# An encoder layer with product-key experts: the dense tokens' queries and scores move from the f32r scores stage to 16 f32 tiles at the head of the expert phase

## What is computed

```python
q = (h @ wq).reshape(nb, L, 8, 256)                 # 8 heads
q1, q2 = q[..., :128], q[..., 128:]
s1 = einsum('blhd,kd->blhk', q1, keys1)             # 128 keys each
s2 = einsum('blhd,kd->blhk', q2, keys2)
v1, i1 = top_k(s1, 16); v2, i2 = top_k(s2, 16)
cand = v1[..., :, None] + v2[..., None, :]          # 256 sums
sc, ci = top_k(cand, 16)
e = i1[ci // 16] * 128 + i2[ci % 16]                # expert of 16384
w = softmax(sc)
act = gelu(einsum('td,tjd->tj', h, u_tab[e]))       # 8 x 16 experts a token
y = einsum('tj,tjd->td', w * act, v_tab[e])
```

## Time and profile before

| | |
|---|---|
| median of 3 runs | 3317.74 us (3316.46 to 3320.41) |
| the profiled execution | 3320.53 us |
| its span in the profile | 3318.8 us |
| TensorE busy | 2949.9 us, 89% |
| VectorE busy | 2375.7 us, 72% |
| ScalarE, GpSimd busy | 545.1 us, 16%; 1227.4 us, 37% |
| DMA | 909.23 MB, mean 274 GB/s |
| mean granted TensorE clock | 0.939 |

### The profile page before, as it was taken

The page is one execution under the profiler, slowest core; times in us unless marked ns, Lnnn a source line. Parts: engine busy times, 40 slices in busy tenths (PEclk is TensorE's granted clock), DMA queues, the critical chain, the costliest instruction groups (busy, mean ns, idle before and its releaser), DMA issues. The chain is left out here.

```text
span 3318.8 us, 31146 instructions
## 1 busy us (share of the span) xinstructions
PE 2949.9 (89%) x10524; PEld 1623.4 (49%) x10524; DVE 2375.7 (72%) x4478; ACT 545.1 (16%) x652; POOL 1227.4 (37%) x1104
## 2 busy tenths in 40 slices
PE   6999689669699769898999999997799999999995
PEld 2457577547488424444444444443344444444442
DVE  4795454621588899999989988876577676776774
ACT  3011443311211112212212221220000000000003
POOL 0111111022111353334444455554465455555560
PEclk8998899779799779999999999999899999999997
...
GB/s 188 177 161 23 58 39 26 32 58 127 45 83 67 229 305 316 342 336 331 365 373 363 370 368 414 413 413 410 389 403 400 401 402 400 402 399 402 400 381 148
DMA packets 296804, 909.23 MB, mean 274 GB/s; under 512 B 26832, under 2 KB 76240, under 8 KB 293584
## 3 DMA queue, kind: packets, MB, share of 16 engines
...
...
## 5 line engine op out<-in xcount | busy, mean ns | idle before, releaser
L1441 PE MATMUL s_pu<-s_hn,s_ut 128*128 128x512 f32 x2048 | 906.6, 599 | 0.0
L1397 POOL DMA_INDIRECT s_slot<-in_u,s_row x512 | 514.8, 1006 | 625.7 <-DVE s_slot L1761 503.8
L1397 POOL DMA_INDIRECT s_slot<-in_v,s_row x512 | 560.1, 1094 | 489.3 <-DVE s_hB L1774 333.3
L1761 DVE SCALAR_TENSOR_TENSOR s_slot<-s_slot,s_ph 128x1024 f32<-128x1024 f32 x512 | 609.0, 1220 | 112.5 <-DMA s_slot<-in_u,s_row 95.6
L1774 DVE SCALAR_TENSOR_TENSOR s_hB<-s_slot,s_dot,s_hB 128x1024 f32<-128x1024 f32 x445 | 561.4, 1284 | 129.0 <-DMA s_slot<-in_v,s_row 128.1
L1441 PEld LDWEIGHTS s_pu<-s_hn,s_ut 128*128 128x128 f32 x2048 | 393.1, 193 | 482.4 <-issue 482.4
L296 PE MATMUL s_ps<-hn_hi,w_hi 128*128 128x512 f32 x832 | 340.9, 410 | 93.5 <-PEq L270 57.2
L297 PE MATMUL s_ps<-hn_lo,w_hi 128*128 128x512 f32 x832 | 332.2, 399 | 0.0
L1513 PE MATMUL s_pw<-s_ct,s_vt 128*128 128x512 f32 x512 | 250.2, 613 | 37.2 <-DMA s_vt<-in_v 20.5
L300 PE MATMUL s_ps<-hn_hi,w_lo 128*128 128x512 f32 x832 | 261.9, 397 | 0.0
L1513 PE MATMUL s_ph<-s_ct,s_vt 128*128 128x512 f32 x512 | 242.6, 597 | 19.5 <-DVE s_slot L1761 19.5
...
## 6 DMA issues: line engine op xcount, KB each, us to landing
s_ut<-in_u_tiles SPq DMA_DIRECT2D x128, 512.0 KB, 7.3
s_vt<-in_v SPq DMA_DIRECT2D x128, 512.0 KB, 24.0
s_g<-s_gst ACTq DMA_DIRECT2D x128, 256.0 KB, 7.0
...
```

The source lines that it names most:

```text
L1397: pool.indirect_dma_start(out=slot[s][:, :], out_offset=None, in_=io[kind], in_offset=bass.IndirectOffsetOnAxis(ap=row[b][:, j:j + 1], axi ...
L1441: mm = pe.matmul(pu[:, n % 2, :], ut[n % UR][:, k, :], hn[:, k, :], start=(k == 0), stop=(k == DC - 1))
L1761: dve.scalar_tensor_tensor(s, s, 1.0, ph[:, :], ALU.mult, ALU.mult, accum_out=dot[b][:, j:j + 1]).then_inc(taken, 1)
```

## The change

`project` gets `halves`; the scores stage calls it with half 0 alone, so that queries, scores, stores and VectorE's copies cover the 512 gathering tokens only. `MADE_PICKS` falls from 4 to 2: in the scores stage VectorE makes the picks of blocks 0 and 1. The queries of the dense tokens are computed at the head of the first expert phase: `QT` = 16 more tiles, n = -16 to -1, use the rings, PSUM and semaphores of the u tiles with `wq` as the weight (plain f32, 8 matmuls). ScalarE copies a query out (`dense_query`), TensorE multiplies its four blocks with the keys (`dense_scores`, one tile later), ScalarE copies and stores the scores (`take_scores`). SP's loads of scores wait until these 16 stores have landed. The blocks are ranked in another order, and the tables of numbers that set rates and places are new. The last eight steps of block 1's ranking, one a tile, lie in tiles -12 to -5.

```diff
@@ -291 +291 @@
-def project(pe, out, w_hi, w_lo, x_hi, x_lo, ks=range(DC)):
+def project(pe, out, w_hi, w_lo, x_hi, x_lo, ks=range(DC), halves=range(2)):
@@ -294 +294 @@
-        for h in range(2):
+        for h in halves:
@@ -1023,2 +1023,3 @@
-    q = [at(f"s5_q{s}", [P, T], F32, F0 + s * 4 * KB) for s in range(2)]
-    sc = at("s5_sc", [P, 2, NB, KEYS], F32, F0 + 8 * KB)
+
+    q = [at(f"s5_q{s}", [P, HALF], F32, F0 + s * 4 * KB) for s in range(2)]
+    sc = at("s5_sc", [P, 2, SPARSE, KEYS], F32, F0 + 8 * KB)
@@ -1028,2 +1029,2 @@
-        ps = [ctx.enter_context(nc.psum_tensor(f"s5_ps{s}", [P, T], F32)) for s in range(2)]
-        pk = [ctx.enter_context(nc.psum_tensor(f"s5_pk{s}", [P, T], F32)) for s in range(2)]
+        ps = [ctx.enter_context(nc.psum_tensor(f"s5_ps{s}", [P, HALF], F32)) for s in range(2)]
+        pk = [ctx.enter_context(nc.psum_tensor(f"s5_pk{s}", [P, HALF], F32)) for s in range(2)]
@@ -1049 +1050 @@
-            for b in range(NB):
+            for b in range(SPARSE):
@@ -1062 +1063 @@
-                    project(pe, ps[s], w.hi[s], w.lo[s], m.hn_hi, m.hn_lo).then_inc(w.used, 1)
+                    project(pe, ps[s], w.hi[s], w.lo[s], m.hn_hi, m.hn_lo, halves=(0,)).then_inc(w.used, 1)
@@ -1077 +1078 @@
-                act.dma_start(m.scores[:, :, bass.ds(h * 2 + s, 1), :].rearrange("b p c k -> p (b c) k"),
+                act.dma_start(m.scores[0:SPARSE, :, bass.ds(h * 2 + s, 1), :].rearrange("b p c k -> p (b c) k"),
@@ -1108 +1109 @@
-                    dve.tensor_copy(sc[:, s, :, :], pk[s][:, :].rearrange("p (b k) -> p b k", b=NB))\
+                    dve.tensor_copy(sc[:, s, :, :], pk[s][:, :].rearrange("p (b k) -> p b k", b=SPARSE))\
@@ -1186,2 +1187,3 @@
-RANKED = (0, 1, 4, 5, 6, 2, 7, 3)
-MADE_PICKS = 4
+RANKED = (0, 1, 4, 5, 2, 6, 3, 7)
+MADE_PICKS = 2
+QT = 2 * PH
@@ -1207,4 +1209,4 @@
-RANK_AT, RANK_TILES, LAST_STEPS = 12, 20, 4
-HOT_AT = (10, 38, 66, 94)
-HOT_TILES = 24
-SIDE_AT, SIDE_TILES = 46, 78
+RANK_AT, RANK_TILES = 2, 16
+HOT_AT = (21, 47, 73, 101)
+HOT_TILES = 22
+SIDE_AT, SIDE_TILES = 26, 98
@@ -1225 +1227 @@
-        return (i - 1) * LAST_STEPS + (x - 24) * LAST_STEPS // 8
+        return 4 - QT + x - 24
@@ -1236,2 +1238,3 @@
-    for t in range(n + 1):
-        tenths += 44 if t < HOT_AT[0] else 34 if t < RANK_AT + RANK_TILES * (len(RANKED) - MADE_PICKS) else 51
+    for t in range(-QT, n + 1):
+        tenths += (45 if t < RANK_AT else 42 if t < HOT_AT[0] else
+                   26 if t < RANK_AT + RANK_TILES * (len(RANKED) - MADE_PICKS) else 47 if t < 123 else 60)
@@ -1263,0 +1267 @@
+    sd = [at(f"s6_sd{s}", [P, NB - SPARSE, KEYS], F32, F0 + 32 * KB + 2 * KB * s) for s in range(2)]
@@ -1316,0 +1321 @@
+        sd_made, sd_taken, sd_stored = sem("s6_sd_made"), sem("s6_sd_taken"), [sem(f"s6_sd_stored{s}") for s in range(2)]
@@ -1339,4 +1344,5 @@
-            for n in range(KEYS):
-                if n >= UR:
-                    sp.wait_ge(u_done, n - UR + 1)
-                sp.dma_start(ut[n % UR][:, :, :], io["u_tiles"][n]).then_inc(u_in[n % UR], 16)
+            for n in range(-QT, KEYS):
+                i = n + QT
+                if i >= UR:
+                    sp.wait_ge(u_done, i - UR + 1)
+                sp.dma_start(ut[n % UR][:, :, :], io["wq"][i] if n < 0 else io["u_tiles"][n]).then_inc(u_in[n % UR], 16)
@@ -1346,0 +1353,2 @@
+                            for s in range(2):
+                                sp.wait_ge(sd_stored[s], 16 * QT // 2)
@@ -1349,0 +1358 @@
+
@@ -1366 +1375 @@
-                    sp.wait_ge(u_done, KEYS)
+                    sp.wait_ge(u_done, QT + KEYS)
@@ -1437,3 +1446,4 @@
-                pe.wait_ge(u_in[n % UR], 16 * (n // UR + 1))
-                if n >= 2:
-                    pe.wait_ge(gelu_done, n - 1)
+                i = n + QT
+                pe.wait_ge(u_in[n % UR], 16 * (i // UR + 1))
+                if i >= 2:
+                    pe.wait_ge(gelu_done, i - 1)
@@ -1444,0 +1455,9 @@
+            def dense_scores(i):
+                pe.wait_ge(gelu_done, i + 1)
+                if i >= 2:
+                    pe.wait_ge(sd_taken, i - 1)
+                for b in range(NB - SPARSE):
+                    c = slice(b * P, (b + 1) * P)
+                    mm = pe.matmul(pw[:, i % 2, c], gst[i % 2][:, c], m.keysT[:, i % 2, :], start=True, stop=True)
+                mm.then_inc(sd_made, 1)
+
@@ -1446 +1465,3 @@
-                if unit >= 2:
+                if unit < 2:
+                    pe.wait_ge(sd_taken, QT - 1 + unit)
+                else:
@@ -1486,0 +1508,2 @@
+                if -QT < n <= 0:
+                    dense_scores(n + QT - 1)
@@ -1508 +1531 @@
-                            pe.wait_ge(gelu_done, KEYS)
+                            pe.wait_ge(gelu_done, QT + KEYS)
@@ -1534 +1557 @@
-                act.wait_ge(u_done, n + 1)
+                act.wait_ge(u_done, QT + n + 1)
@@ -1536,0 +1560,2 @@
+                else:
+                    act.wait_ge(sd_made, QT + n - 1)
@@ -1538 +1563 @@
-                act.wait_ge(gelu_done, n + 1)
+                act.wait_ge(gelu_done, QT + n + 1)
@@ -1540,0 +1566,16 @@
+            def dense_query(i):
+                act.wait_ge(u_done, i + 1)
+                if i >= 2:
+                    act.wait_ge(sd_made, i - 1)
+                act.activation(gst[i % 2][:, :], pu[:, i % 2, :], ACT.Copy).then_inc(gelu_done, 1)
+
+            def take_scores(i):
+                act.wait_ge(sd_made, i + 1)
+                if i >= 2:
+                    act.wait_ge(sd_stored[i % 2], 16 * (i // 2))
+                act.activation(sd[i % 2][:, :, :], pw[:, i % 2, :].rearrange("p (b k) -> p b k", k=KEYS), ACT.Copy)\
+                   .then_inc(sd_taken, 1)
+                act.wait_ge(sd_taken, i + 1)
+                act.dma_start(m.scores[SPARSE:NB, :, i, :].rearrange("b p k -> p b k"), sd[i % 2][:, :, :])\
+                   .then_inc(sd_stored[i % 2], 16)
+
@@ -1586,2 +1627,7 @@
-            for n in range(KEYS):
-                gelu_tile(n)
+            for n in range(-QT, KEYS):
+                if n < 0:
+                    dense_query(n + QT)
+                else:
+                    gelu_tile(n)
+                if -QT < n <= 0:
+                    take_scores(n + QT - 1)
@@ -1592 +1638 @@
-                    if n > 1 and sparse_by(n - 2) <= number["u", b, P - 1] < sparse_by(n - 1):
+                    if sparse_by(n - 2) <= number["u", b, P - 1] < sparse_by(n - 1):
@@ -1912 +1958 @@
-    m.picks = [Picks(m, (R0 + 104 * KB + 4608 * s) if s < 3 else F0 + 59 * KB + 512, s) for s in range(MADE_PICKS)]
+    m.picks = [Picks(m, R0 + 104 * KB + 4608 * s, s) for s in range(MADE_PICKS)]
```

## The result

The changed kernel took 3279.82 us, median of three runs (3275.08 to 3280.21), against 3317.74 before: ratio 0.9879, 95% interval 0.9861 to 0.9897. The forecast was 3272, range 3238 to 3304. Four more runs of the same kernel, made with the last experiments, gave 3287.12 (3285.17 to 3289.76) against 3317.80, ratio 0.9905 (0.9890 to 0.9920). The profiled execution took 3279.82 us, its span is 3278.1.

What follows compares the result with a forecast made beforehand. TensorE paced the scores stage; VectorE's slots, stretched at the end by transfers, set the first expert phase. Scores stage -111, first expert phase +69, second -3: -45 on 3320.5, 3275.5, or 3272 for the median; range 3238 to 3304.

Steps and rivals of the forecast that it cites:

- Scores stage, -111: Scores stage: TensorE's matmuls halve, eight pairs of tiles save 100 us and the tail behind the last scores 11 more.
- The pair was put at 12.8: Scores stage: a pair of tiles falls from 25.35 to 12.8 us, 0.2 of it for a new wait.
- just inside: Scores stage: VectorE's work for a pair, two half-size copies and two heads of 4.89, takes some 12 us.
- VectorE's slots and the head, +139.8: First expert phase before the tail: VectorE's slots grow from 809 to 931.8 us, +122.8, and the head adds +17.
- the tie of 680 against 664 us: First expert phase, tiles 21 to 97: TensorE has 680 us of work, VectorE 664, so either's delay shows.
- The +17 of the head: First expert phase, tiles -16 to 1: transfers of 136 us, not VectorE's 110, set the length; +17 taken.
- The tail, -70.5: End of the first expert phase: transfers at 413 GB/s fall from 147 MB in 355 us to 118 MB in 285.
- TensorE's waits: First expert phase: TensorE's waits for one-hots and side rows under 60 us together; above 79 us would be wrong.
- the slower rival: First expert phase: TensorE's new 123.8 us stay in series, its 89.4 us of waits remain; 3328 us, chance 0.05.
- SP now holds two loads of scores until all 16 stores have landed: First expert phase, tile 2: VectorE is then behind TensorE, so the held loads cost nothing; uncovered up to 10 us.
- a sign of being wrong: First expert phase, tile 2: a wait of VectorE for scores beyond 10 us would show the prediction wrong.

Runs made afterwards that it cites:

- experiment 2: The change with the picks of four blocks, 0 to 3, made in the scores stage instead of two; 3380.6 us.
- experiment 1: The change with the 16 new query tiles issuing one TensorE matmul of 128x512 instead of eight; 3283.8 us.
- experiment 6: The change with tiles 24 to 127 of the first expert phase doing one of their eight matmuls; 3285.4 us.
- experiment 7: The change with gathering rates raised in tiles 98 to 127, so all 512 rows of u are done in the first phase; 3289.9 us.
- experiment 9: The change itself, unaltered, run four more times beside the last experiments; 3287.1 us.
- experiment 10: The change with 3.5 gathered rows a tile in tiles -16 to 1, not 4.5, higher rates later, all 512 rows of u done; 3291.1 us.
- experiment 3: The change with the earlier kernel's gathering rates and side rows from tile 46; 3328.9 us.
- experiment 4: The change with block 2 ranked early, in tiles -10 to 6, and new tables of rates and places; 3264.1 us.
- experiment 5: The change with every key-tile matmul in the scores stage executed twice on the same half; 3378.2 us.
- experiment 8: The version of experiment 4 with block 2 ranked in tiles -10 to 8, other tables and all 512 rows of u; 3269.0 us.
- experiment 12: The version of experiment 4 with side rows from tile 34 instead of 23 and all 512 rows of u done; 3275.3 us.
- experiment 11: The version of experiment 8 with side rows in tiles 34 to 123 instead of 25 to 123; 3271.7 us.

## Why the prediction was right, step by step

**Scores stage, -111.** Measured -110.5. The pair was put at 12.8 and is 12.76. The remark that VectorE stays "just inside" was true but thin: experiment 2 shows that GpSimd's remainders can stretch four additions of VectorE from 0.41 to 4.64 us, which my count of VectorE's instructions left out. In the change the same additions took 1.21 us at 945.24, beside a remainder at 943.76, and the pair still fitted.

**VectorE's slots and the head, +139.8.** From the phase's start to the end of tile 91 before took 863.3 us (to 1960.16), to the end of tile 97 after 1005.3 (to 1991.66): +142.0. The number is right, but the reading under it, that the phase's length is the sum of VectorE's slots, holds in the change for the first part alone. Up to tile 16 the time goes by VectorE: TensorE's 96 us less gave nothing (experiment 1). From tile 16 to 96 it goes by TensorE: 85 us less of VectorE change nothing (experiment 2), TensorE emptied gives back 16 us (experiment 6). The sum of VectorE's slots fitted there because the two are so near, the tie of 680 against 664 us that the forecast had named itself; that a sum over VectorE alone came out within 2 us is in part luck. The +17 of the head stood on transfers of 136 us beside 138 of TensorE. Dense tiles are 7.76 us apart (7.7 forecast), and with TensorE's part taken out tile 0 comes 28 us earlier (experiment 1), so the tiles of the head are TensorE's; the gathered rows are not, as VectorE's 81st ends at 165 us in the change and at 177 in experiment 1.

**The tail, -70.5.** Measured -69.0: 364.6 us before (1960.16 to 2324.79), 295.6 after (1991.66 to 2287.22), at 413 GB/s. Experiments 6 and 7 support the cause: less TensorE work doesn't shorten it, and four more rows lengthen the phase by 8 us.

**TensorE's waits.** For one-hots and side rows 19.1 us (under 60 forecast), before the first turn 14.7, VectorE's for rows 85.0 (under 95.6). So the new 123.8 us of TensorE work stand against 55.6 us of waits that it no longer has and a phase that is 73 us longer, 8.5 of which are a longer wait for the first product; the slower rival needed waits of 79 us or more.

**Where it was off.** The step "SP now holds two loads of scores until all 16 stores have landed; I take nothing; uncovered it costs up to 10 us" bounded the price wrongly. It holds in the first profile (3.9 us), but was 15.8 in experiment 9, beyond the 10 us that were set as a sign of being wrong, 32.7 in 10 and 71.8 in 3. VectorE is not held to TensorE's tiles in the head, so it is not behind TensorE there but ahead, whenever TensorE is late or rows are few. And no term stood for the stop of the head, which costs the kernel some 8 us at the first product. Both series lie 8 and 15 us above the 3272 forecast and inside the range. The second wait at the second phase's start stood in no term either (19.5 us before, at 2351.99, and 16.0 now); by experiments 7 and 4 it is a matter of how many rows of u are left over.

**Still open.** Why ScalarE and SP see TensorE's count up to 11 us late in the head. The stop of 8 us or more at tile 0 was in all five later profiles without an early block (experiments 5, 6, 7, 9 and 10), and not in the first profile nor in experiments 2 to 4. Experiments 1 to 4, 5 to 8 and 9 to 12 ran on three different chips, and the traces of the last two lack events, so a part of the chip or of the tracing in it can't be excluded. Nor was a version tried in which GpSimd's remainders keep clear of VectorE's additions, which by the last pair of experiment 2 would take 4 us off each pair there.

**The best version** is the early ranking of experiment 4 or 8. Beside the change in one series, experiment 11 (of that family) is 15.5 us faster, 3271.7 against 3287.1, with intervals of the ratios that don't meet (0.9834 to 0.9865, 0.9890 to 0.9920).
